# Order of the queues in a mixer step: scans split and set later, gated rows ahead, exponentials and query products moved back

## What is computed

```python
def gated_delta_rule(q, k, v, g, beta):          # 4 heads x 128
    gc   = cumsum(g)                             # inside a chunk
    m    = where(strict, (k_beta @ k.T) * decay, 0)
    u, w = solve(I + m, [v_beta, k_beta * exp(gc)])   # unit lower triangular
    # over chunks: v_new = u - w @ state;  o = q_dec @ state + attn_intra @ v_new
    #              state = state * chunk_decay + k_dec.T @ v_new

def hgrn2_recurrence(q, k, v, log_f):            # 4 heads, 64 x 64 state
    bcum  = cumsum(log_f)                        # "running sums"
    o     = (q * exp(bcum)) @ state + scores @ v
    # scores[t,s] = sum_k q[t,k] * exp(bcum[t,k] - bcum[s,k]) * k[s,k],  s <= t
    state = exp(last)[:, None] * state + (k * exp(last - bcum)).T @ v
```

## Time and profile before

| | |
|---|---|
| median of three runs | 1379.13 us |
| profiled execution | 1385.77 us |
| its span, first to last instruction | 1384.0 us |
| mean granted TensorE clock | 0.983 |
| PE busy | 1333.4 us (96%) |
| DVE, ACT, POOL busy | 783.5, 592.7, 674.3 us |
| chain that ended last, share of PE | 86% |
| key_state of step 0 to that of step 7 | 460.16 to 628.18 us |

### The profile page before, as it was taken

How to read it: one execution, slowest core, us unless ns; L and a number is a source line. 1 busy time by engine, 2 the same in 40 slices (tenths; PEclk the granted TensorE clock), 3 DMA queues, 4 the chain that set the end, 5 groups by cost and what they waited for, 6 DMA issues and landing times.

```text
span 1384.0 us, 24260 instructions
## 1 busy us (share of the span) xinstructions
PE 1333.4 (96%) x9101; PEld 1106.9 (80%) x9101; DVE 783.5 (57%) x1171; ACT 592.7 (43%) x1403; POOL 674.3 (49%) x583
## 2 busy tenths in 40 slices
PE   5999999999999998888999999999999999999997
PEld 4777887978888777767888788888888888788886
DVE  5014635557354488984147965655555556665657
ACT  6234535445343466662133433333333334344445
POOL 3224324133253477760300876676666677754442
PEclk9999999999999799998999999999999999999999
DMA  5131322323225342514210244554555545876653
GB/s 184 33 105 51 97 62 87 119 73 118 66 78 137 103 128 83 188 57 157 61 31 1 84 151 149 157 160 149 171 175 155 164 145 206 310 267 197 190 191 122
DMA packets 160371, 178.60 MB, mean 129 GB/s; under 512 B 9520, under 2 KB 110464, under 8 KB 160256
## 3 DMA queue, kind: packets, MB, share of 16 engines
q1 hardware_dynamic: 160112, 176.53, 39.9%
q10 hardware_dynamic: 144, 0.52, 0.1%
HBM read 124.32 MB, written 52.71 MB: 128 GB/s over the span
## 4 chain that ended last, share of the span: by engine, by line
PE 86%; DVE 5%; issue 3%; POOL 2%; ACT 1%; DMA 1%; SPq 0%; DVEq 0%; ACTq 0%; POOLq 0%
PE banks L2416 9%; PE banks L2418 9%; PE banks L2417 9%; PE banks L353 6%; PE banks L355 6%; PE banks L354 6%; PE banks L2427 4%; PE banks L2428 4%; PE banks L2429 4%; PE banks L692 2%; PE banks L693 2%; PE banks L694 2%; PE banks L2108 2%; PE banks L2110 2%; PE banks L2109 2%
## 5 line engine op out<-in xcount | busy, mean ns | idle before, releaser
L2574 POOL TENSOR_TENSOR w_l<-area,w_h 128x512 fp32r<-128x512 f32 x119 | 175.4, 1479 | 180.2 <-ACT w_h L2469 135.0
L2574 POOL TENSOR_TENSOR w_l<-w_raw,w_h 128x512 fp32r<-128x512 f32 x100 | 140.4, 1405 | 99.8 <-ACT w_h L2524 50.3
L353 PE MATMUL banks<-act_h,w_h 128*128 128x512 f32 x352 | 141.4, 402 | 0.0
L355 PE MATMUL banks<-act_h,w_l 128*128 128x512 f32 x352 | 137.6, 391 | 0.0
L354 PE MATMUL banks<-act_l,w_h 128*128 128x512 f32 x352 | 137.2, 390 | 0.0
L341 POOL TENSOR_TENSOR w_l<-w_raw,w_h 128x1024 fp32r<-128x1024 f32 x24 | 59.4, 2478 | 142.5 <-ACT w_h L334 125.3
L2416 PE MATMUL banks<-act_h,w_h 128*128 128x512 f32 x320 | 124.5, 389 | 0.0
L2417 PE MATMUL banks<-act_l,w_h 128*128 128x512 f32 x320 | 124.5, 389 | 0.0
L2418 PE MATMUL banks<-act_h,w_l 128*128 128x512 f32 x320 | 124.5, 389 | 0.0
L2427 PE MATMUL banks<-w_h,act_h 128*128 128x512 f32 x308 | 120.1, 390 | 0.4 <-DVE act_l L2726 0.4
L2428 PE MATMUL banks<-w_l,act_h 128*128 128x512 f32 x308 | 119.8, 389 | 0.0
(11 more groups left out here) (316 smaller groups left out, 3347.2 us busy)
## 6 DMA issues: line engine op xcount, KB each, us to landing
w_raw<-in_w_in SPq DMA_DIRECT2D x22, 512.0 KB, 3.9
w_raw<-in_w_gate SPq DMA_DIRECT2D x22, 512.0 KB, 4.5
area<-in_w_up SPq DMA_DIRECT2D x22, 512.0 KB, 4.6
ff_wide<-in_w_down SPq DMA_DIRECT2D x22, 512.0 KB, 4.2
down_sums<-ff_wide SPq DMA_DIRECT2D x11, 1024.0 KB, 4.1
area<-in_x SPq DMA_DIRECT2D x8, 1024.0 KB, 7.9
projected_tm<-area SPq DMA_DIRECT2D x32, 256.0 KB, 2.4
hidden_sums<-area SPq DMA_DIRECT2D x6, 1024.0 KB, 4.2
```

The costliest lines, as they stand in the source:

```text
L353: e.matmul(dst, w_h[:, b, k], act_h[:, k, cols], start=(k == 0), stop=False)
L355: mm = e.matmul(dst, w_l[:, b, k], act_h[:, k, cols], start=False, stop=(k == KT - 1))
L2574: e.tensor_tensor(slot(w_l, u), raw_use(u) if u < NU_FF else wd_raw(u - NU_FF), slot(w_h, u).bitcast(F32), ALU.subtract).then_inc(sems["fl ...
```

## The change

On ACT: out_high goes from the end of the step to between inverse(u,1) and high(s,0); inverse(u,3) goes ahead of to_end(u); spans(u,0,3) goes behind high(s,1), and spans(u,3,4) behind keys_turned(t). On DVE: running is split by group; final_hg(s) and update(u,1) go ahead of the first scan; pack(u,2) goes ahead of gated_state(s); update(u,2) and the second scan follow it, and take(t,0) comes behind them. queries 0 to 2 go behind pack(u,6), and query 3 behind final_dn(t). For tile 0 the two scans still stand together. No instruction is added or removed, and the queues of PE, POOL and SP keep their order.

```diff
--- before.py
+++ after.py
@@ -1654,34 +1654,34 @@
                     new_values(t)
                 if live(u):
                     inverse(u, 1)
+                if 0 <= t < 4:
+                    out_high(e, 0, t)
                 if live(s):
                     high(s, 0)
                 if live(u):
                     from_start(u)
                 if live(u):
                     inverse(u, 2)
-                    spans(u, 0, 3)
+                    inverse(u, 3)
                 if live(u, NT - 1):
                     to_end(u)
-                if live(u):
-                    inverse(u, 3)
                 if live(s):
                     high(s, 1)
                 if live(u):
-                    spans(u, 3, 4)
+                    spans(u, 0, 3)
                     inverse(u, 4)
                 if live(t):
                     squares(t)
                     lengths(t)
                 if live(t, NT - 1):
                     keys_turned(t)
+                if live(u):
+                    spans(u, 3, 4)
                 if live(v):
                     decays(v)
                 if live(u):
                     inverse(u, 5)
                     whole_inverse(u)
-                if 0 <= t < 4:
-                    out_high(e, 0, t)
 
             def beside(unit):
                 if unit == 0:
@@ -1769,14 +1769,14 @@
                 e.scalar_tensor_tensor(out=hls[:, :, :], in0=hin[:, c % 2, 2:4, :], scalar=0.0, in1=hls[:, :, :],
                                        op0=ALU.min, op1=ALU.subtract).then_inc(sems["f_log"], 1)
 
-            def running(c):
-                e.wait_ge(sems["f_log"], c + 1)
-                reach(e, "h_dl", 2 * NX * c)
-                reach(e, "kde", 2 * c)
-                reach(e, "eb", c)
-                reach(e, "h_bk", c)
-                for g in range(2):
-                    e.tensor_tensor_scan(hb[:, g, :], ones[:, :], hls[:, g, :], 0.0, ALU.mult, ALU.add).then_inc(sems["h_b"], 1)
+            def running(c, g):
+                if g == 0:
+                    e.wait_ge(sems["f_log"], c + 1)
+                    reach(e, "h_dl", 2 * NX * c)
+                    reach(e, "kde", 2 * c)
+                    reach(e, "eb", c)
+                    reach(e, "h_bk", c)
+                e.tensor_tensor_scan(hb[:, g, :], ones[:, :], hls[:, g, :], 0.0, ALU.mult, ALU.add).then_inc(sems["h_b"], 1)
 
             def take(c, lv):
                 e.wait_ge(sems["h_p"], 4 * c + lv // 2 + 1)
@@ -1860,20 +1860,21 @@
                     residual(t)
                 if live(u):
                     pack(u, 1)
-                    running(u)
                 if t == NT:
                     out_add(e, 1)
                 if live(s):
                     final_hg(s)
                 if live(u):
                     update(u, 1)
+                    running(u, 0)
+                    pack(u, 2)
                 if live(s, NT - 1):
                     gated_state(s)
+                if live(u):
+                    update(u, 2)
+                    running(u, 1)
                 if live(t):
                     take(t, 0)
-                if live(u):
-                    pack(u, 2)
-                    update(u, 2)
                 if live(t):
                     take(t, 1)
                 if live(u):
@@ -1885,13 +1886,11 @@
                 if live(t):
                     take(t, 3)
                 if live(u):
-                    queries(u, 0)
                     pack(u, 4)
                 if live(s):
                     low(s, 0)
                 if live(u):
                     update(u, 4)
-                    queries(u, 1)
                 if live(t):
                     final_sb(t)
                     take(t, 4)
@@ -1906,13 +1905,13 @@
                     update(u, 5)
                 if live(t):
                     take(t, 6)
-                if live(u):
-                    queries(u, 2)
                 if live(t):
                     take(t, 7)
                 if live(u):
                     pack(u, 6)
-                    queries(u, 3)
+                    queries(u, 0)
+                    queries(u, 1)
+                    queries(u, 2)
                 if live(t):
                     final_dn(t)
                 if t == NT - 1:
@@ -1920,6 +1919,7 @@
                         e.wait_ge(sems[f"x_loaded{n}"], 32)
                     out_add(e, 0)
                 if live(u):
+                    queries(u, 3)
                     queries(u, 4)
                     queries(u, 5)
                     queries(u, 6)
@@ -1943,7 +1943,8 @@
                     log_sigmoids(0)
                     pack(0, 2)
                     update(0, 2)
-                    running(0)
+                    running(0, 0)
+                    running(0, 1)
                 if unit == 2:
                     pack(0, 3)
                     update(0, 3)
```

## The result

Over six executions the changed kernel takes 1388.95 us (1386.78 to 1393.39), the kernel before in the same job 1379.57 (1377.30 to 1385.66): ratio 1.0052 [1.0029, 1.0075], which is 7 us by the ratio and 9.4 between the medians. It is slower, by less than the 1% that was set as "no change"; the forecast was 1387, and the range held it.

The account below looks back on a forecast made before the run. TensorE was taken to bound the whole kernel (96% busy), with PE and DVE at 89% each in the mixer loop. Steps 1 to 5 +11.8, step 0 +1.4 and step 6 -5.4 gave +7.8 us: 1387, range 1376 to 1408.

Parts of the forecast that it names:

- What DVE and POOL do to each other: Shared ports: a DVE product of two SBUF tiles waits until POOL's current instruction ends; PSUM readers keep their times.
- Late key_sums: POOL, step 1: key_sums needs both scans, so it starts about 7.4 us behind key_state instead of 3.6.
- m_turn: PE, steps 1 to 3: m_turn comes late with with_decay and waits from 513.2 to 516.1, 2.9 us.
- Steps 1 to 3: Mixer loop: 22.39 us plus 3.4 from the late with_decay, 25.8 us each.
- Steps 4 and 5: Mixer loop without out_low: with_decay 1.25 us late, 23.65 us each.
- Step 6: final_sb and update(u,5) come earlier and the clock need not fall: -5.4 us, or -1.7 if it falls.
- Step 0: out_low starts 2.13 us earlier and holds the third query; key_state of step 1 comes 1.4 us later.
- The sum: Whole kernel: +11.8 for steps 1 to 5, +1.4 and -5.4 give +7.8 us, median 1387.
- clock: Rival, chance 0.30: PE's waits before m_turn in steps 1 to 3 lower the clock; 1398 to 1417 us, middle 1407.
- The head: Start of each step: final_hg and update(u,1) ahead of the scans; 22.39 us pattern in all, against an average of 22.57.
- Locks miss: Rival, chance 0.16: POOL and DVE drift or collisions share, each step loses 0.3 to 0.5 us; about -4, 1375.
- faster: Rival, chance 0.04: earlier turn(u,1) and pack(u,2) carry through, PE's waits go in all steps; 1364 us.

Follow-up runs that it names:

- after: The changed kernel itself, with the whole change against the kernel before: 1388.95 us, ratio 1.0052.
- scans together: Changed kernel with the second scan, running(u, 1), moved up right behind the first, ahead of pack(u,2): 1393.73 us, ratio 1.0085.
- step-6 wait: Kernel before with one wait added: in step 6 alone POOL starts gates only when final_sb is done; 1375.59 us, ratio 0.9956.
- experiment 5: Changed kernel with all seven query products placed behind final_dn, which reads PSUM: 1387.38 us, ratio 1.0028.

## Why the prediction was right

**What DVE and POOL do to each other** held, and carried the forecast. The products end just behind out_low where they meet it, 0.15 us in step 2 of after and with the scans together, and behind its first half when it is halved. By the trace the lock of the Trainium skill (SBUF — State Buffer, "Who interferes with whom") is right here, against a shared slowdown: three queries took 3.69 us, not the 1.8 that three at 0.60 would.

**Late key_sums**: forecast 7.4 us behind key_state, read 8.64 in step 1, where the clock was low, and 7.18 in step 2 (520.21 against 513.03). **final_sb**: forecast 1.9, read 1.72 and 1.71. **out_low free of ACT, and one query behind it**: yes. **m_turn**: forecast 2.9 us late in steps 1 to 3, read 2.83 in step 2, and 1.35 and 0.22 in steps 1 and 3, where PE was slow. **Steps 1 to 3**: forecast 25.8; step 2, the undisturbed one, 25.49; steps 1 and 3 came to 27.11 and 26.37 with the clock low in them. **Steps 4 and 5**: forecast 23.65, read 23.35. **Step 6**: the forecast of -5.4 was -3.9 inside the step and -1.5 behind it. Read: -4.2 inside, and -1.6 behind it (from key_state of step 7 to the next matmul of L1326 8.84 us before, 628.18 to 637.02, and 7.27 after, 631.80 to 639.07). Steps 1 to 5 together are 125.67 against the forecast 124.7; that closeness is luck, since without the low clock of steps 1 and 3 they would be about 123.2.

**Step 0** was sized wrong: +1.4 forecast, about +2.4 at the high clock. There out_low (480.63 to 483.03) caught not the third query but one of the four behind final_dn, DVE row first:

```profile
478.48 2.33 DVE L1718 TENSOR_TENSOR area<-area 128x128 f32<-128x128 f32 x3
480.73 1.11 DVE L1833 SCALAR_TENSOR_TENSOR area<-banks,r_dn,area 128x128 f32<-128x128 f32 x4
481.77 2.01 DVE L1718 TENSOR_TENSOR area<-area 128x128 f32<-128x128 f32 x4
```

```profile
479.57 1.09 POOL L1975 TENSOR_TENSOR area<-area,vbs 128x512 f32<-128x512 f32 x1
480.63 2.40 POOL L667 TENSOR_TENSOR w_l<-w_raw,w_h 128x1024 fp32r<-128x1024 f32 x1
```

**The sum** was drawn up against a profile that held a fall of the clock in step 0 (7.2 us, 30.78 against 23.54) and was taken over to the median as it stood. From key_state of step 0 to that of step 7 the loop is 171.86 us in after. In before it is 168.02, and 160.8 without that fall: +11.1. Of this, 2.5 us are the low clock of steps 1 and 3 of after (1.6 and 0.9 above step 2). So the waits and locks of the forecast are worth +8.6 in the loop, where the forecast had +11.8 + 1.4 - 3.9 = +9.3: the tail was 0.3 too long in each step, step 0 was 1.0 too short. The low clock, for which the sum had nothing, brings it back up. With the 1.6 that comes back behind the loop this gives +9.5, and the medians differ by 9.4. Which falls of the clock the median executions hold is not known, so the agreement to a fraction of a microsecond is luck; the mechanism is not.

One of its own signs of being wrong came true: it named a granted clock below 1.00 in these steps, and steps 1 and 3 ran at 0.84 and 0.81. So part of the **clock** rival took place beside the forecast. Two falls came behind m_turn's waits of 2.59 and 2.83 us, as it had it, and two behind the waits for update(u,5), where it had none. They were short, and steps 3 and 1 are 0.9 and 1.6 us longer than step 2, not the 10 that it took for one fall. At the low clock PE is behind DVE, which hides the wait: m_turn waits 0.22 us in step 3. The Trainium skill (TensorE: Matmul & The Clock Gate, "Why this matters for your kernels") warns of idle gaps between bursts. The trace has falls behind both of these gaps, and others behind waits of 1.13 and 1.08 us. The prediction read rows 4 as a wait of 1.96 us that does no harm, and overlooked that before had its longest fall behind a wait of 1.90 at 464.2.

**The head**: I credited it with 22.39 in all steps. The prediction assumed that gain. In the changed kernel no run shows it by itself; the head with both scans together, on the kernel before, gives 4.7 us on top of the step-6 wait. What the split of the scans takes from it by itself was not measured apart from out_low. **Locks miss** and **faster** are refuted: the changed kernel is slower, and m_turn waits. With out_high back, what "locks miss" asked for is built by hand, and even then the ratio is 0.9998 and not the 0.997 of its 1375 us: its step 2 loses 1.1 us, not 0.3 to 0.5.

## What to carry to other kernels

In these traces an instruction of VectorE with two inputs in SBUF waited for the whole GpSimd instruction that was running (up to 2.4 us for a product of 0.28), and one with an input in PSUM did not. So put the first kind where GpSimd idles, keep the second for where it is busy, and look at what a GpSimd instruction that is freed earlier will now run beside. When a producer is put behind other work (here the second scan), count to the last consumer down the other engine's queue; the reorder of the head paid only once both scans kept their early place. Compare stretches at the same granted clock before comparing totals: here one fall of the clock in one execution was worth 7 us, as much as the change.

## What was not expected of the hardware

The same wait does not always bring the same clock. In step 0, 4.1 us behind key_state (464.2 in before), PE waits 1.89 or 1.90 us in all these profiles. In those of before and of the halved out_low the clock from 468 to 472 was 0.50, and the step took 30.78 and 31.22 us. In after's it was 1.00 there, and in all but those two the step took 23.5 to 26.3. Of the stretches with 1.08 and 0.53 us of waiting, one fell to 0.50 and another stayed at 1.00. What tells them apart is open.

Once GpSimd is ahead, VectorE gets in about once per instruction of GpSimd, whatever the length of that one: the four multiplies of final_sb beside spreads of about 0.48 us took 1.71 to 1.81 us in steps 1 to 5 of after, the three queries beside one of 0.7, one of 1.1 and one of 2.4 us took 4.09 (scans together). Once VectorE is ahead it is GpSimd that waits, for a whole row of short products: the seven queries and the out_low of 3.66 us in experiment 5. There 0.5 us of order, 0.05 ahead against 0.44 behind, decided between 1.50 and 3.27 us. Instructions with an input in PSUM kept their times: final_dn 1.10 beside values, with_decay 1.11 or 1.12 in the steps shown.
